# Query/key products and one output-gate tile ahead of the S5 input, a turned scan in two halves, and GpSimd scaling three mLSTM heads

## The reference

```python
proj = xn @ w_in
u, xm, v, o_pre = jnp.split(proj, [S5_WIDTH, S5_WIDTH + ML_WIDTH, S5_WIDTH + 2 * ML_WIDTH], axis=-1)
y_a = s5_group(u, ...)              # a_bar = exp(lam*dt); states_t = a_bar*states_(t-1) + b_bar*u_t
xc = silu(causal_dwconv(xm, ml_conv_w, ml_conv_b))
q = einsum('bshd,hde->bshe', xc, ml_w_q); k = einsum('bshd,hde->bshe', xc, ml_w_k)
gates = concat([q, k, vh]) @ ml_w_gates + ml_b_gates
h_t = rmsnorm(mlstm_chunkwise(q, k, vh, gates[..., :4], gates[..., 4:]), ml_norm_g)
y_b = sigmoid(o_pre) * h_t
return concat([y_a, y_b]) @ w_out
```

## Time and profile before

| | us |
|---|---|
| median of 3 runs | 1124.43 |
| the runs | 1121.94, 1124.43, 1125.12 |
| the profiled execution, whole | 1122.38 |
| its span, first to last instruction | 1120.6 |
| PE busy | 1091.4 (97%) |
| DVE busy | 653.1 (58%) |
| ACT busy | 463.2 (41%) |
| POOL busy | 211.9 (19%) |

### The profile page before, as it was taken

One profiled execution on the slowest core, in us unless ns is written; L12 is line 12 of the kernel. 1 busy time (PEld: TensorE's weight loads), 2 busy tenths in 40 slices (PEclk: granted clock), 3 DMA queues, 4 the chain that ended last, 5 costly groups with the idle time before them and its releaser, 6 DMA issues.

```text
span 1120.6 us, 15490 instructions
## 1 busy us (share of the span) xinstructions
PE 1091.4 (97%) x5542; PEld 883.0 (79%) x5542; DVE 653.1 (58%) x871; ACT 463.2 (41%) x671; POOL 211.9 (19%) x312
## 2 busy tenths in 40 slices
PE   9968998999999999999999999999999999999997
PEld 8857646888888888888888777778888888888886
DVE  6698773556666666653333666366666666652333
ACT  6424554454434443433323465454434434432221
POOL 7998991040000000000000022030000000000000
PEclk9988999999999999999999999999999999999999
DMA  6541300422322222232323211042222322223322
GB/s 221 168 94 58 93 6 1 169 94 95 106 99 94 94 94 94 95 111 94 113 96 128 71 55 58 30 133 101 94 94 94 103 103 94 94 94 113 97 92 75
DMA packets 36491, 106.73 MB, mean 95 GB/s; under 512 B 7840, under 2 KB 10144, under 8 KB 36320
## 3 DMA queue, kind: packets, MB, share of 16 engines
q1 hardware_dynamic: 36448, 106.15, 28.6%
HBM read 101.55 MB, written 3.15 MB: 93 GB/s over the span
## 4 chain that ended last, share of the span: by engine, by line
PE 84%; DVE 1%; ACT 1%; issue 0%; DVEq 0%
PE bank L1433 26%; PE bank L1435 26%; PE bank L1434 26%; PE bank L1775 1%; PE bank L1456 1%; PE bank L1797 1%; PE bank L1595 1%; PE bank L1628 0%; PE bank L1629 0%; PE bank L1568 0%; PE bank L1575 0%; DVE xlo L968 0%; PE bank L1589 0%; DVE outb L1414 0%; PE bank L1453 0%
## 5 line engine op out<-in xcount | busy, mean ns | idle before, releaser
L1433 PE MATMUL bank<-xhi,whi 128*128 128x512 f32 x992 | 390.2, 393 | 3.2 <-DVE xlo L1199 2.8
L1434 PE MATMUL bank<-xlo,whi 128*128 128x512 f32 x992 | 386.2, 389 | 0.0
L1435 PE MATMUL bank<-xhi,wlo 128*128 128x512 f32 x992 | 386.2, 389 | 0.0
L962 DVE TENSOR_TENSOR wlo<-raw,whi 128x1024 fp32r<-128x1024 f32 x177 | 223.1, 1261 | 207.7 <-ACT whi L645 207.0
L645 ACT ACTIVATE whi<-raw 128x1024 fp32r<-128x1024 f32 x177 | 187.0, 1057 | 350.5 <-PE bank L1435 321.8
L1433 PEld LDWEIGHTS bank<-xhi,whi 128*128 128x128 f32 x992 | 186.2, 188 | 45.8 <-issue 5.8
L1434 PEld LDWEIGHTS bank<-xlo,whi 128*128 128x128 f32 x992 | 186.2, 188 | 39.2 <-issue 1.0
L1435 PEld LDWEIGHTS bank<-xhi,wlo 128*128 128x128 f32 x992 | 186.2, 188 | 38.8
L1433 PE MATMUL bank<-ahi,whi 128*128 128x512 f32 (+1 forms) x374 | 142.5, 381 | 0.0
L1435 PE MATMUL bank<-ahi,wlo 128*128 128x512 f32 (+1 forms) x374 | 141.6, 379 | 0.0
L1434 PE MATMUL bank<-alo,whi 128*128 128x512 f32 (+1 forms) x374 | 140.4, 375 | 0.0
(11 more groups left out here) (235 smaller groups left out, 1099.7 us busy)
## 6 DMA issues: line engine op xcount, KB each, us to landing
raw<-wstream SPq DMA_DIRECT2D x177, 512.0 KB, 3.3
xin<-xT SPq DMA_DIRECT2D x8, 256.0 KB, 5.5
raw<-wstream SPq DMA_DIRECT2D x8, 256.0 KB, 5.0
h<-xT SPq DMA_DIRECT2D x1, 2048.0 KB, 8.6
outT<-outb SPq DMA_DIRECT2D x8, 256.0 KB, 2.2
u_scratch<-uperm SPq DMA_DIRECT2D x1, 1024.0 KB, 5.7
uc<-u_scratch SPq DMA_DIRECT2D x8, 128.0 KB, 4.9
bcp<-bc SPq DMA_DIRECT2D x1, 512.0 KB, 5.3
```

The lines of the kernel that those rows point to most:

```text
L962: V.tensor_tensor(wlo[:, t % RING, :], raw[:, t % RAWS, :], whi[:, t % RING, :].bitcast(f32), ALU.subtract).then_inc(lo_done, 1)
L1433: MM(dst, wh, rhi, start=start, stop=False)
L1434: MM(dst, wh, rlo, start=False, stop=False)
L1435: return MM(dst, wl, rhi, start=False, stop=stop)
```

## The change

Seven things, all in layer 0's mixer.

1. PE forms queries and keys and gate tile 13 right after tile 11, ahead of the transposes of gg. The gate logits lie between the two halves of the transposes, the S5 convolution kernel ahead of the S5 input, and gate tiles 14 and 15 follow each other.
2. DVE makes pieces 1 to 4 of gg in one stretch after tile 11's evacuation, and POOL 5 to 7. The low parts of tiles 13 and 14 stand ahead of tile 11's evacuation on DVE. ACT copies the queries (DVE did).
3. Many of DVE's operations have an operand or a result in a PSUM bank instead of SBUF: the convolution's accumulator, the powers q, one of the two products of g_step and read_out.
4. POOL carries a second set of columns through the pole computation (the pole's turning without its decay, so 2 x 32 columns where 2 x 16 were), builds from it a table turn of 32 chunks' rotations, multiplies the S5 input by it backwards, and multiplies the result forwards again (turned_by).
5. Between the two, the recurrence has a real factor: four tensor_tensor_scan on DVE (turned_half), two halves of 32 chunks, real and imaginary part, with a carry that POOL adds.
6. POOL clears toep (ACT did), makes read-outs 6 and 7 and the skip rows, and after the scan scales the outputs of heads 0 to 2 and takes their low parts (DVE did).
7. ACT negates c and fills cdiag (POOL and DVE did), loads the GELU table ahead of the third S5 output, and takes head 3's high part ahead of the GELU. The gathers of uc stand one ahead of each of the loads 11 to 14 and four behind load 15, where two stood ahead of each of the first four.

```diff
+        def gather(s):
+            src = u_scratch.rearrange("m (g i) s c -> i (m g) s c", i=GCH)[:, :, CH - 1 - s, :]
+            sp.dma_start(uc[s * GCH:(s + 1) * GCH, :, :], src).then_inc(u_back, 16)
         for t in range(11, 15):
-            for s in (2 * (t - 11), 2 * (t - 11) + 1):
-                src = u_scratch.rearrange("m (g i) s c -> i (m g) s c", i=GCH)[:, :, CH - 1 - s, :]
-                sp.dma_start(uc[s * GCH:(s + 1) * GCH, :, :], src).then_inc(u_back, 16)
...
+        W, M, PP, Tt, Uu, C = (sm[:, k:k + 4, :].rearrange("p (r k) j -> p r (k j)", r=2)
+                               for k in (2, 6, 10, 14, 18, 22))
+        pole, turning = slice(0, PAIRS), slice(PAIRS, 2 * PAIRS)
...
+        for s in range(5, CH):
+            g_step(s, gg[:, :, :, 0:GCH], qq[:, 0, s - 1, pole], qq[:, 1, s - 1, pole], g_built)
...
+        Z, Tz, Uz, radii = qq[:, :, CH - 1, turning], Tt[:, :, turning], Uu[:, :, turning], C[:, 0, turning]
+        tt(Tz, Z, Z, ALU.mult)
+        settle()
+        tt(Uz[:, 0, :], Tz[:, 0, :], Tz[:, 1, :], ALU.add)
+        settle()
+        ts(Uz[:, 0, :], Uz[:, 0, :], -0.5, ALU.mult, 1.5, ALU.add)
+        settle()
+        tt(turn[:, :, :, 0], Z, both(Uz[:, 0, :]), ALU.mult)
+        settle()
+        tt(Tz, turn[:, :, :, 0], qq[:, :, CH - 1, pole], ALU.mult)
+        settle()
+        G.tensor_tensor(radii, Tz[:, 0, :], Tz[:, 1, :], ALU.add).then_inc(radius_done, 1)
+        n = 1
+        while n < HALF_CH:
...
         pool.wait_ge(mean_done, 1)
...
+        for s in (6, 7):
+            tt(T5, CC, wide(qq[:, 0, s, pole]), ALU.mult)
+            tt(U5, CC, wide(qq[:, 1, s, pole]), ALU.mult)
+            settle()
+            slot = slice(s * GCH, (s + 1) * GCH)
+            tt(ff[:, 0, :, slot], T5[:, 0], U5[:, 1], ALU.add)
+            G.tensor_tensor(ff[:, 1, :, slot], T5[:, 1], U5[:, 0], ALU.subtract).then_inc(f_last, 1)
+            pool.wait_ge(f_last, s - 5)
...
+        def turned_by(dst, src, back):
+            tt(tprod[:, :, :, :], src, turn[:, 0:1, :, :].to_broadcast([P, 2, PAIRS, HALF_CH]), ALU.mult)
+            tt(uprod[:, :, :, :], src, turn[:, 1:2, :, :].to_broadcast([P, 2, PAIRS, HALF_CH]), ALU.mult)
+            settle()
+            tt(dst[:, 0], tprod[:, 0], uprod[:, 1], ALU.add if back else ALU.subtract)
+            return G.tensor_tensor(dst[:, 1], tprod[:, 1], uprod[:, 0], ALU.subtract if back else ALU.add)
+        part = [xs[:, :, :, HALF_CH * b:HALF_CH * (b + 1)] for b in range(2)]
+        pool.wait_ge(k_ready, 1)
+        pool.wait_ge(s5in_copied, 2)
+        for b in range(2):
+            turned_by(xr[:, b], part[b], True).then_inc(turned, 1)
+            pool.wait_ge(turned, b + 1)
+            settle()
+        end, head = xr[:, 0, :, :, HALF_CH - 1], xr[:, 1, :, :, 0]
...
+        pool.wait_ge(turned_scan, 2)
+        product(end, jump[:, 0, :], jump[:, 1, :], Tz, Uz)
+        tt(Tz[:, 0, :], Tz[:, 0, :], Uz[:, 1, :], ALU.subtract)
+        tt(Tz[:, 1, :], Tz[:, 1, :], Uz[:, 0, :], ALU.add)
         settle()
...
+        G.tensor_tensor(head, head, Tz, ALU.add).then_inc(carry_done, 1)
+        for b in range(2):
+            pool.wait_ge(turned_scan, 2 * b + 2)
+            turned_by(part[b], xr[:, b], False).then_inc(scan_done, 1)
+            pool.wait_ge(scan_done, b + 1)
             settle()
...
+        G.memset(toep[:, :, :, :], 0.0).then_inc(toep_clear, 1)
+        for hd in range(HEADS - 1):
+            pool.wait_ge(num_gated, hd + 1)
+            pool.wait_ge(hfac_done, hd + 1)
+            G.tensor_tensor(hb[:, hd % 2, :], hb[:, hd % 2, :], dsq[:, hd % 2, :], ALU.mult).then_inc(o_scaled, 1)
+            pool.wait_ge(ybhi_done, hd + 1)
+            G.tensor_tensor(xlo[:, 4 + hd, :], hb[:, hd % 2, :], xhi[:, 4 + hd, :].bitcast(f32),
+                            ALU.subtract).then_inc(yb_done, 1)
...
+        act.wait_ge(bc_in, 16)
+        A(bcp[:, 3, :], bcp[:, 3, :], ACT.Copy, scale=-1.0).then_inc(c_negated, 1)
+        for t in range(1, 10):
             split_hi(t + RING)
...
+        split_hi(T_QK + 2)
+        for hd in range(HEADS):
+            act.wait_ge(qk_ready, hd + 1)
+            A(qT[:, hd, :], bank[QK_BANK[hd]][:, :], ACT.Copy).then_inc(q_evac, 1)
+        split_hi(T_QK + 3)
...
         head_factor(HEADS - 1)
+        act.preload_act_table_set("gelu_apprx_tanh_and_others")
         s5_output(2)
+        head_hi(HEADS - 1)
         s5_gelu(0)
...
+        t5, u5 = gtmp, bank[5][:, :].rearrange("p (r j i) -> p r j i", r=2, i=GCH)
+        qp = bank[4][:, 0:2 * SUP * PAIRS].rearrange("p (r k j) -> p r k j", r=2, j=PAIRS)
...
+        def turned_half(n):
+            b, r = n // 2, n % 2
+            dve.wait_ge(radius_set, 1)
+            dve.wait_ge(turned, b + 1)
+            if b:
+                dve.wait_ge(carry_done, 1)
+            x = xr[:, b, r, :, :].rearrange("p j c -> p (j c)")
+            V.tensor_tensor_scan(x, bank[1][:, :], x, 0.0, ALU.mult, ALU.add).then_inc(turned_scan, 1)
...
             else:
                 if m == 0:
                     dve.wait_ge(u_saved, 16)
+                if m == 3:
+                    split_lo(T_QK + 1)
+                    split_lo(T_QK + 2)
+                    wait_tile_used(dve, t)
...
+        dve.wait_ge(g0_done, 1)
+        dve.wait_ge(q_done, 1)
+        dve.wait_ge(out_freed, 7)
+        steps.up(V.tensor_copy(qp, qq[:, :, :, 0:PAIRS]))
+        settle()
+        for step in range(1, 5):
...
+        turned_half(0)
+        turned_half(1)
...
         weights(0)
+        turned_half(2)
         weights(1)
+        turned_half(3)
+        split_lo(T_O + RING)
         out_gate(3)
         for hd in range(HEADS):
...
             if hd == 0:
-                split_lo(T_O + 3 + RING)
+                split_lo(T_O + 1 + RING)
             if hd >= 2:
-                head_scale(hd - 2)
-                head_lo(hd - 2)
+                split_lo(T_O + hd + RING)
             weights(SB * hd + 3)
-            if hd == 0:
-                read_out(6)
             if hd + 1 < HEADS:
                 weights(SB * (hd + 1))
```

More of the change, by code:

```diff
@@ L61 @@
 RAWS, RING = 2, 4
-IN_BANK = (0, 1, 2, 3, 4, 5, 6, 0, 1, 2, 3, 0, 1, 2, 3, 0, 1, 2, 3, 0)
+IN_BANK = (0, 1, 2, 3, 4, 5, 6, 0, 1, 2, 3, 0, 1, 2, 3, 0)
+QK_BANK = (1, 2, 3, 0)
+E_WIDTH = tuple(SEQ - P * s for s in range(SB))
+E_AT = tuple(sum(E_WIDTH[:s]) for s in range(SB))
 COLS = {}
@@ L507, in _ @@
         ts(qq[:, 1, 0, :], M[:, 1, :], 1.0, ALU.mult)
-        product(M, lr, ni)
-        tt(C[:, 0, :], Tt[:, 0, :], Uu[:, 1, :], ALU.subtract)
-        tt(C[:, 1, :], Tt[:, 1, :], Uu[:, 0, :], ALU.add)
+        Tp, Up, Cp, Pp = (x[:, :, pole] for x in (Tt, Uu, C, PP))
+        product(M[:, :, pole], lr, ni, Tp, Up)
+        tt(Cp[:, 0, :], Tp[:, 0, :], Up[:, 1, :], ALU.subtract)
+        tt(Cp[:, 1, :], Tp[:, 1, :], Up[:, 0, :], ALU.add)
         pool.wait_ge(s5_recip, 1)
         settle()
-        tt(PP, C, both(den), ALU.mult)
+        tt(Pp, Cp, both(den), ALU.mult)
         settle()
@@ L747, in decay @@
                 act.wait_ge(w_done, SB * (hd - 1) + s + 1)
-            A(ebuf[:, s, P * s:], bank[2][:, P * s:], ACT.Exp, bias=acol[:, s, hd:hd + 1]).then_inc(e_done, 1)
+            A(ebuf[:, E_AT[s]:E_AT[s] + E_WIDTH[s]], bank[2][:, P * s:], ACT.Exp, bias=acol[:, s, hd:hd + 1]).then_inc(e_done, 1)
         def head_squares(hd):
@@ L1098, in _ @@
-        read_out(4)
+        read_out(0, qr, ur)
+        read_out(1, qr, ur)
+        dve.wait_ge(gates_ready, 1)
+        V.tensor_scalar(g8[:, :], bank[0][0:104, :], col("bgate", 0, 104), None, ALU.add).then_inc(gates_copied, 1)
+        for step in range(2, 5):
+            read_out(step, qr, ur)
+        split_lo(T_QK + 3)
+        split_lo(T_QK + RING)
+        read_out(5, qs, rtmp[:, 1])
+        dve.wait_ge(kt_ready, 1)
+        V.tensor_copy(ksb[:, :, :], bank[6][:, :].rearrange("p (g i) -> p g i", i=GCH)).then_inc(k_copied, 1)
@@ L1495, in _ @@
             ins.then_inc(m1_ready, 1)
+        pe.wait_ge(con_in, 16)
+        pe.wait_ge(out_freed, 7)
+        pe.wait_ge(g_built, CH - 5)
+        pe.wait_ge(g_mid, 4)
+        for b in range(4):
+            s5_in_turned(b)
+        pe.wait_ge(k_evac, HEADS)
+        for k in range(12):
+            q = k % 4
+            ins = MM(bank[0][32 * q:32 * q + 8, :], cols("wg")[:, 8 * k:8 * k + 8],
+                     (qT, kT, vT)[k % 3][:, k // 3, :], start=k < 4, stop=k >= 8)
+        ins.then_inc(gates_ready, 1)
+        for b in range(4, 8):
+            s5_in_turned(b)
+        pe.wait_ge(cdiag_set, 2)
+        for jb in range(4):
+            for r, g in enumerate((gre, gim)):
+                for q in range(4):
+                    j = 4 * jb + q
+                    ins = MM(bank[3][32 * q:32 * q + 32, jb * P:(jb + 1) * P],
+                             cdiag[:, r, j, :, :].rearrange("p f i -> p (f i)"), g[:, j, :],
+                             start=jb == 0 and r == 0, stop=jb == 3 and r == 1)
+        ins.then_inc(k_ready, 1)
```

(8 more changed lines are left out.)

379 lines of the change are left out of this document (156 added, 223 removed).

## The result

The changed kernel takes 1112.1 us (median of 4 executions, 1110.96 to 1113.7) against 1123.4 for the kernel before in the same session; the ratio is 0.990, with a 95% interval of 0.988 to 0.992. It is faster by 11.3 us. The prediction was 1103, its range ended at 1110: too optimistic by 9 us, and outside. The profiled execution took 1110.96 (span 1109.2, mean granted clock 0.995), where the sum on record gave 1102.0.

The account below looks back on a forecast made before the run. PE, busy 97% of the span, was taken as the bound, so gain came from its waits and low clock. Terms -12.5 - 2.5 - 1.3 + 0.5 - 2.5 + 0.3 - 2.4 = -20.4 gave 1102.0, put at 1103 us; range 1098.5 to 1110.

Parts of the forecast that it names:

- the rows chain on DVE: Gate rows between S5 input and head 0: acol copied at 113 to 115, PE at 113.8; 0.5 us new wait.
- Gap before the S5 input: PE's 12.8 us wait for gg goes but for 0.3: -12.5; the low clock after it goes too: -2.5.
- (a): Rival: DVE's chain for gg is late because the bank does not free the convolution from POOL; 1105.5 us, chance 0.17.
- POOL's pole computation: Ahead of gg's pieces: doubled columns cost about +4 us, pieces end near 78.5, 6 us in time.
- (d): Rival: POOL's pole computation grows in proportion to its columns, PE waits 38.5 us at gg's transposes; 1144 us, chance 0.03.
- the two waits of 0.3 that the sum kept: Before the S5 input: 0.3 us of PE's wait kept for gg and 0.3 for ACT's copy of v.
- Heads: Waits for the next weights: 2.5 of 2.9 us given back as DVE's scaling and low parts move to POOL.
- The 0.3 (0 to 3): Head 0: cost of POOL's long products beside DVE's SBUF-only masking of ebuf, 0.3 us taken, range 0 to 3.
- Rival (b): GpSimd blocks DVE in the heads, so nothing is gained there; 1106 us, chance 0.17.
- GLU: Ahead of the GLU: earlier table load and high part free DVE for the GELU part, -2.4 us (-1.5 to -2.8).
- The scan: The S5 scan's replacement ends at 128 to 138 us, before PE wants it at 158; nothing lost.
- (e): Rival: the turned chain is late for the S5 outputs and replaces the gap; about 1113 us, chance 0.03.

Follow-up runs that it names:

- e3: The changed kernel with the convolution's accumulator back in SBUF instead of the bank, nothing else; 1116.8 us.
- e10_mask_bank: e8 with the masks of heads 0 and 1 made on the scores in their bank, nothing left out; 1101.7 us, ratio to before 0.981.
- e5: The changed kernel with ACT rounding two output weight tiles ahead of a head's factor instead of behind it; 1112.5 us.
- e2: The changed kernel with GpSimd's backward turning passes on 2 of 32 chunks, states not the reference's; 1106.1 us.
- e7: The changed kernel with read-out 5 and the gate rows' operands in banks, one split and acol moved; 1106.9, 1107.0, 1111.7, 1111.8 and 1112.6 us.
- e11: The order of e7 with read-out 5 in a bank, but the rows of the gates in SBUF as in the changed kernel; 1110.0 us.
- e8: e7 with ACT's order of e5; 1104.9, 1104.9, 1109.9, 1111.0 and 1111.1 us.
- e9: e8 with GpSimd's forward turning passes on 2 of 32 chunks, states not the reference's; 1101.7 us.

## Why the prediction was wrong

The direction and the place of the gain were right; the step that failed is "the rows chain on DVE then takes two splits and one read-out (5 to 7)". It took 13.0, and the gate rows behind it 6.7 for 5. The chain was late although it began early: the sum to "113 to 115" only comes out from 99.6, when PE is there, and DVE began the splits at 97.74. The prediction had read the mutual blocking out of the earlier trace rows, used it for the convolution, and let POOL's turning passes "start when the S5 input is copied, at 98"; it never laid the one beside the other, though both stood at 98 in its own working, and it charged the passes' neighbourhood to head 0 alone. Point by point:

- Gap before the S5 input: right. -12.5 and its low clock -2.5 came as put. Convolution steps took 2.34 each time (2.4 on record), so (a) did not occur; e3 prices them at 4.7 us. The pieces of gg took 2.18 in a bank (the free pace, as chosen; the upper end of the range did not occur) and ended at 84.55 for 84.1.
- POOL's pole computation: right, with room. Its pieces began at 59.4 instead of 62 and ended at 73.9 instead of 78.5; (d) is ruled out.
- Rows chain: "0.5 us of new wait (0 to 1.2)" was 5.04 + 0.62 + 0.24 = 5.9. And a wait of that size costs the clock, for which no term stood: from arow's transposes to head 0 the changed kernel took 12.13 us, 11.27 without its two waits, e10_mask_bank 8.37; 2.9 us. With 5.4 of excess wait that is 8.3 against the 7.5 missed at head 0. Of the other 0.8, 0.6 are the two waits of 0.3 that the sum kept, at gg's transposes and for v's copy; neither stands among PE's waits. The rest was not traced. The 2.9 are those of this execution (1.4 more in e5's, with the same program up to there). e2 shows the cause by taking the passes away, e7 against e11 by the operands of the rows alone; e11 also shows that the order, with a split ahead of the rows, was the larger part.
- Heads: -2.5 + 0.3 was -0.4. In the changed kernel the waits of 0.84 and 0.48 us at 137 and 139 are head 0's and 1's masks beside the forward passes (one took 2.44); of the 0.99 at 162.69, 0.36 is ACT's order, since the rounding of a tile at 158.13 stood ahead of the squares at 159.07 (e5). Between the changed kernel and e10 the heads differ by 1.64 us: 1.27 up to the norm of head 0 (16.18 and 14.91 after its start), where the masks lie beside the passes, and 0.37 between the norms of heads 1 and 2, which is ACT's order. The 0.3 (0 to 3) was mis-sized: once head 0 starts on time, the masks cost 3.3 us, and 9 when the clock falls at them (e10 against e8). Rival (b) named this mechanism and priced it at 3 us.
- GLU: right, 2.6 for 2.4.
- The scan: done at 139.45, before the 146 named and 1.5 behind the 128 to 138 worked out; the S5 outputs did not wait for it, so (e) did not occur. toep was issued only from 143.1 on and so was not complete by 146, with no effect on the S5 outputs at 166.5.

With both failures taken out, the sum comes true: the terms put head 0 at 138.08 - 15.8 = 122.3 and the S5 outputs at 157.3; in e10_mask_bank they lie at 122.25 and 157.39, and its time is 1101.7 where 1102.0 to 1103 stood. So the terms together were well sized for a kernel in which DVE is not held up at these two places, with a little luck in how close they come: e10 also has ACT's order (0.37), and a wait of 0.9 for the sixth read-out, for neither of which the sum has a term, and the 0.6 of kept waits did not come. The range failed because (b) was given one place: the same mechanism at a second one, and the clock behind it, were not in it.

The runs give the extent of the blocking: instructions with two inputs in SBUF (splits, masks, scans, the read-out), and nmrow, with one, which is free at 0.41 and took 2.43. This is the rule that the prediction cited for head 0 and did not apply at 98 us; of the instructions it had named only those with two SBUF inputs. The Trainium skill ("SBUF — State Buffer", section "SBUF: two separate sides") calls the shared port pair an exclusive lock, held for a whole instruction, that VectorE takes with two SBUF inputs or in a two-port mode. The runs agree: the waits are as long as a product of POOL (2.4), and nmrow, from SBUF to SBUF, is the kind of instruction that can run in such a mode by that page of the Trainium skill.

Still open is why the clock falls at the same waits in some executions only, and for longer in some than in others.

## What to carry to other kernels

When a change makes GpSimd work on SBUF in a new stretch (clearing a tile aside, which held nobody here), list DVE's instructions there by their operands: those with all inputs in SBUF cost up to a GpSimd instruction's length each, those with one input in a bank their own time. A tile moved to a bank, even four rows of it, can be worth more than the instruction's whole duration, though it has its price: nmrow takes 0.68 from the bank, and 0.41 from SBUF when nothing holds it. Price a new wait of PE with the stretch of low clock that may follow it, and follow a gain through the next stage: here it was given back twice where the work it brought forward met the same neighbour. And before two medians are compared, look whether the times fall into groups with different mean granted clocks: what looked like 2.0 us for ACT's order was 0.36 and the clock.

## What had not been expected of the hardware

- Small instructions are held as long as large ones: nmrow's 4x512 took 2.43 us for 0.41, a 128x128 mask 2.43 for 0.27. It works both ways: POOL's product of 2.35 us took up to 3.4.
- GpSimd's clearing of toep, which only writes, held nobody; the prediction had expected this, and the runs bear it out (in e9 a split beside it took its free 1.23 us). In e10_mask_bank POOL began it at 134.90, and DVE masked in SBUF in the midst of it, in its free time (DVE's timeline, then POOL's):

```profile
136.18 0.28 DVE L1212 SCALAR_TENSOR_TENSOR ebuf<-ebuf,con 128x128 f32<-128x128 f32 x1
```

```profile
134.90 3.51 POOL L642 MEMSET toep<- 128x4096 f32 x1
```

- The clearing took 3.51 us, where the prediction allowed up to 8.5.
- The clock's answer to the same pair of waits (1.7 and 1.5 us, 2.76 of 6 us busy) differs between executions of one program, and with it the time by 5 to 6 us.
- In e11 the clock fell to 0.50 behind a wait of only 0.57 us; in e7, where that wait is gone, it stayed at 1.00 in the same place.
